# Six transformer layers on one core: the indexer's narrow columns share a block with the last values, the memory's values of two layers fill one block, its queries one tile

## The reference, cut to what matters

```python
# kind A; x is (256, 1024), all float32
q, k, v, qi, wi, ki, qm = split_cols(x @ w_in_a[j],
    (MIX_WIDTH, MIX_WIDTH, MIX_WIDTH, IDX_HEADS * IDX_DIM, IDX_HEADS, IDX_DIM, MEM_WIDTH))
...
ki = apply_rope(layer_norm(ki, idx_kn_g[j], idx_kn_b[j])[:, :, None, :], cos, sin)[:, :, 0]
mix = dsa_attention(q, k, heads(v, N_HEADS, HEAD_DIM), qi, wi, ki)
...
mk, mv = jnp.split(mem_n @ w_mem_kv[i], 2, axis=-1)
mo = memory_attention(heads(qm, ...), mk..., mv...)
mixed = jnp.concatenate([mix, mo], -1) @ w_out[i]
x = layer_norm(ALPHA * x + mixed, ...)
x = layer_norm(ALPHA * x + swiglu(x, w_gate_up[i], w_down[i]), ...)
```

## Time and profile before

| | us |
|---|---|
| median of 3 runs | 1611.58 (1610.95 to 1612.87) |
| the profiled execution, its own time | 1612.3 |
| its span, first to last instruction | 1610.5 |
| TensorE busy with matmuls | 1579.4 |
| VectorE busy | 1072.7 |
| ScalarE busy | 735.9 |
| mean granted TensorE clock | 0.993 |

### The profile page before, as it was taken

One profiled execution on the slowest core, in us unless ns is written; L12 is line 12 of the kernel. 1 busy time (PEld: TensorE's weight loads), 2 busy tenths in 40 slices (PEclk: granted clock), 3 DMA queues, 4 the chain that ended last, 5 costly groups with the idle time before them and its releaser, 6 DMA issues. The chain is left out here.

```text
span 1610.5 us, 20186 instructions
## 1 busy us (share of the span) xinstructions
PE 1579.4 (98%) x8390; PEld 1325.2 (82%) x8390; DVE 1072.7 (67%) x1403; ACT 735.9 (46%) x897; POOL 48.9 (3%) x89
## 2 busy tenths in 40 slices
PE   8999999999999999999999999999999999999998
PEld 6998888888878888888888888888888878887986
DVE  5784776756657767475766666766776668666754
ACT  5435444443434444345444443554444434564472
POOL 1100000000000000000000000000100000000000
PEclk9899999999999999999999999999999999999999
DMA  8552367564515666443367564522676546334530
GB/s 326 195 194 79 127 239 273 219 227 159 206 53 196 237 259 235 183 161 127 122 240 272 220 231 147 179 101 105 253 275 239 211 154 230 145 117 158 197 131 26
DMA packets 45179, 299.89 MB, mean 186 GB/s; under 512 B 5460, under 2 KB 5716, under 8 KB 11552
## 3 DMA queue, kind: packets, MB, share of 16 engines
q1 hardware_dynamic: 38880, 278.48, 46.6%
q0 software_dynamic: 5776, 19.01, 3.7%
q10 hardware_dynamic: 432, 1.11, 0.2%
HBM read 296.20 MB, written 2.65 MB: 186 GB/s over the span
## 5 line engine op out<-in xcount | busy, mean ns | idle before, releaser
L958 PE MATMUL psum<-w_high,xt_high 128*128 128x512 f32 (+2 forms) x1472 | 576.3, 392 | 10.6 <-DVE xt_low L1493 5.1
L1467 DVE TENSOR_TENSOR w_low<-w_raw,w_high 128x2048 fp32r<-128x2048 f32 (+1 forms) x240 | 544.5, 2272 | 44.9 <-ACT w_high L1287 43.7
L960 PE MATMUL psum<-w_high,xt_low 128*128 128x512 f32 (+2 forms) x1472 | 566.4, 385 | 0.0
L959 PE MATMUL psum<-w_low,xt_high 128*128 128x512 f32 (+2 forms) x1472 | 565.9, 384 | 0.0
L1287 ACT ACTIVATE w_high<-w_raw 128x2048 fp32r<-128x2048 f32 (+1 forms) x240 | 456.8, 1905 | 238.0 <-DMA w_raw<-in_weights 158.5
L958 PEld LDWEIGHTS psum<-w_high,xt_high 128*128 128x128 f32 x1472 | 279.1, 190 | 66.7 <-DVE w_low L1467 6.3
L960 PEld LDWEIGHTS psum<-w_high,xt_low 128*128 128x128 f32 x1472 | 279.0, 190 | 55.7
L959 PEld LDWEIGHTS psum<-w_low,xt_high 128*128 128x128 f32 x1472 | 279.3, 190 | 51.0
L1761 DVE TENSOR_TENSOR arena<-arena,psum 128x256 f32<-128x256 f32 x88 | 37.0, 420 | 206.5 <-ACT arena L1378 206.1
L958 PE MATMUL psum<-w_high,ht_high 128*128 128x512 f32 x352 | 140.8, 400 | 0.0
L960 PE MATMUL psum<-w_high,ht_low 128*128 128x512 f32 x352 | 137.5, 391 | 0.0
(11 more groups left out here) (230 smaller groups left out, 1608.8 us busy)
## 6 DMA issues: line engine op xcount, KB each, us to landing
w_raw<-in_weights SPq DMA_DIRECT2D x262, 1024.0 KB, 4.8
norm_params<-in_ln_g POOLq DMA_DIRECT2D x8, 512.0 KB, 4.1
norm_params<-in_ln_b POOLq DMA_DIRECT2D x8, 512.0 KB, 5.7
w_raw<-in_weights SPq DMA_DIRECT2D x4, 512.0 KB, 7.7
kv_outside<-arena POOLq DMA_DIRECT2D x3, 512.0 KB, 5.0
mem_kv<-kv_outside POOLq DMA_DIRECT2D x3, 512.0 KB, 3.7
norm_params<-mods_outside POOLq DMA_DIRECT2D x3, 512.0 KB, 5.8
x_rows<-in_x SPq DMA_DIRECT2D x2, 512.0 KB, 5.7
```

What stands on the lines that cost most here:

```text
L958: e.matmul(dst, a_hi, b_hi, start=first, stop=False)
L959: e.matmul(dst, a_hi, b_lo, start=False, stop=False)
L960: return e.matmul(dst, a_lo, b_hi, start=False, stop=last)
L1467: e.tensor_tensor(K.w_lo[:, s, 0:w], K.w_raw[:, r, 0:w], K.w_hi[:, s, 0:w].bitcast(F32), ALU.subtract).then_inc(K.taken.hit(t), 1)
```

## The change

1. In kind A the 72 narrow columns are laid beside the last 256 columns of the values: "beside", 328 columns, two tiles of 128 x 1312, at the place of narrow (line 595; in layer 3 line 603). VectorE copies the 8 and the 64 columns out as before, then ScalarE copies the 256 values (to two spare places in layer 0), and only that frees the bank.
2. The tail of kind A is gone. Its memory queries are one tile, "queries" (256 columns for all 1024 inputs), multiplied where the tail's turned half was; VectorE copies them out.
3. The memory's blocks are by pairs of layers, (1, 2) and (3, 0): a block of keys, 256 columns of each layer, turned, and a block of values, 512 columns wide with the rows standing, copied out in two instructions. The parks of layers 1 and 2 stand behind the first pair.
4. In kind A the attention's first unit starts a round earlier relative to the gemms (no step ahead in `headed`), and the transposes of the mix stand behind a round of units, not behind the gemm.

```diff
-BOTH = ("turned", "memory", "tail")
+BOTH = ("turned", "memory", "tail", "queries")
+BESIDE = MEMW + IDX_H + HD
+PAIRS = ((1, 2), (3, 0))
...
-        for layer in (*range(1, len(KINDS)), 0):
-            uses = [self.gemms.take() for _ in range(2)]
-            for half in range(2):
-                t = self.tile("w_mem_kv", layer, 0, "half", 4 * half)
...
+        for pair in PAIRS:
+            for part, sort in (("keys", "memory"), ("values", "block")):
+                uses = [self.gemms.take() for _ in range(2)]
+                for half in range(2):
+                    t = self.tile("w_mem_kv", pair, part, "pair", 4 * half)
+                    for n in range(2):
+                        self.gemm(t, n, half, ("mem",), "gemm", uses[n], sort)
+                        if half:
+                            self.evacuate((part, pair))(n, uses[n], t)
...
+        def beside(hooks):
+            uses = [self.gemms.take() for _ in range(RB)]
+            for half in range(2):
+                t = self.tile(w_in, at, None, "beside", 4 * half)
+                for rb in range(RB):
+                    self.gemm(t, rb, half, gen, "gemm", uses[rb], "beside")
+                    if half:
+                        beside_out(rb, uses[rb], t)
+                    hooks[half][rb]()
...
-            narrow([self.memory_rows(0), self.on])
+            beside([[self.on, self.on], [self.memory_rows(0), self.on]])
...
-        units = self.headed(own[0] + own[1][:ahead] + mem[:1] + own[1][ahead:] + mem[1:], 1 - ahead)
+        units = self.headed(own[0] + own[1][:ahead] + mem[:1] + own[1][ahead:] + mem[1:], 1 if kind == "C" else 0)
...
-        some(1, t_tail, ("tail", layer), "tail", [self.on, begin])
+        if kind == "A":
+            some(0, t_tail, ("qm", layer), "queries", [self.on, begin])
+        else:
+            self.blocks[("qm", layer), 0] = some(1, t_tail, ("tail", layer), "tail", [self.on, begin])
         some(0, t, ("proj", layer, 3), "block", [self.on] * 2)
-        some(0, t_tail, ("tail", layer), "tail", [self.on] * 2)
+        if kind != "A":
+            use = some(0, t_tail, ("tail", layer), "tail", [self.on] * 2)
...
         def first_turned():
+            if kind == "A":
+                self.step_background()
             if kind != "B":
                 self.xt(mix, 0, (0,))
-            self.on()
+            self.split() if kind == "A" else self.on()
...
-    if where == ("mem", 3):
+    if where[0] in ("keys", "values") and where[1] == PAIRS[1]:
         engine.wait_ge(*K.parked[1].at(0))
...
+    def evac_ki(j):
+        layer, rb, use, tile = j
+        act.wait_ge(*K.keys_out.at((layer, rb)))
+        e.activation(K.last_values(layer, rb), psum[:, K.gemms.place(use), 0:MEMW],
+                     ACT.Copy).then_inc(K.gemms.sem(use), 1)
```

More of the change, by code:

```diff
@@ L593, in queries, with beside_out @@
             return then
[L595 to L601, removed]
+        def beside_out(rb, use, t):
+            self.blocks[("v", layer), rb] = use
+            self.add("evac_ki", (layer, rb, use, t))
+        def beside(hooks):
[7 more added lines that the diff above has]
+                    hooks[half][rb]()
         def first_columns(more):
             halves = [self.tile(w_in, at, 3 * MIX, "half", 4 * half) for half in range(2)]
-            t, t_more = self.tile(w_in, at, None, "narrow", 0), self.tile(*more[:4], 0)
+            t = [self.tile(w_in, at, None, "beside", 4 * half) for half in range(2)]
+            t_more = self.tile(*more[:4], 0)
             uses_more = []
@@ L669, in attention @@
         self.group([keys], gen, [[self.on, keys_turned(0)], [self.step_background if late else self.on, keys_turned(1)]], True)
-        t_tail, t = [[self.tile(*what[:4], 4 * half) for half in range(2)] for what in (tail, values)]
+        if kind == "A":
+            t_tail = [self.tile(tail[0], tail[1], None, "queries", 0)] * 2
+        else:
+            t_tail = [self.tile(*tail[:4], 4 * half) for half in range(2)]
+        t = [self.tile(*values[:4], 4 * half) for half in range(2)]
         def some(n, tiles, where, sort, hooks):
@@ L1063, in gemm @@
             ring = K.gemms if j.ring == "gemm" else K.wide
-            halves = (0, 1) if j.kind == "narrow" else (j.half,)
-            bank, w = ring.place(j.use), IDX_H + HD if j.kind == "narrow" else BLK
-            if 0 in halves:
+            bank, half = ring.place(j.use), j.half
+            w = {"beside": BESIDE, "queries": SEQ}.get(j.kind, BLK)
+            if half == 0:
                 pe.wait_ge(*ring.free(j.use))
             rows_hi, rows_lo = (K.mt_hi, K.mt_lo) if j.gen[0] == "mem" else (K.xt_hi, K.xt_lo)
-            turned = j.kind == "turned" or (j.kind, rb) in (("memory", 0), ("tail", 1))
@@ L1636, in evac_ki @@
         layer, rb, use, tile = j
-        bank, rows = psum[:, K.gemms.place(use), :], K.idx[:, rb, :]
+        bank, rows = psum[:, K.gemms.place(use), MEMW:BESIDE], K.idx[:, rb, :]
         v.wait_ge(*K.multiplied.at((tile, rb)))
@@ L2241, in width @@
     def width(self, t):
[L2242 removed]
+        return KC // 2 * BESIDE if self.plan.tiles[t].what == "beside" else TW
     def part2(self, c):
@@ L2248, in kv_made, with kv_ready, last_values @@
         return self.kv_later[layer - 1] if layer else self.kv
+    def kv_ready(self, layer):
+        pair = next(pair for pair in PAIRS if layer in pair)
+        return [self.made(("keys", pair), pair.index(layer))] + [self.made(("values", pair), rb) for rb in range(RB)]
+    def last_values(self, layer, rb):
+        if layer == 0:
+            return (self.zeros32, self.ret_s[1][:, 0:MEMW])[rb]
+        return self.proj[:, rb, 4 * BLK:3 * MIX]
     def shift_row(self, layer):
@@ L2360, in pack_weights @@
             own = m[r, cols:cols + BLK]
-        elif what == "narrow":
+        elif what == "pair":
+            c0 = MEMW if cols == "values" else 0
+            own = np.concatenate([inputs[name][n][r, c0:c0 + MEMW] for n in layer], axis=1)
+        elif what == "beside":
             c0 = 3 * MIX + IDX_W
-            own = m[:, c0:c0 + IDX_H + HD]
+            own = np.concatenate([m[r, 4 * BLK:3 * MIX], m[r, c0:c0 + IDX_H + HD]], axis=1)
+        elif what == "queries":
+            own = m[:, m.shape[1] - MEMW:]
         elif what == "up":
```

149 lines of the change are left out of this document (84 added, 65 removed).

## The result

The changed kernel takes 1614.24 us (median of 20 runs, 1611.79 to 1617.16) against 1612.12 of the kernel before (20 runs, 1610.42 to 1614.46): ratio 1.0013 [1.0007, 1.0019], so 0.13% slower, where I had forecast 0.02% faster. Run again beside its variants it took 1615.16 us (11 runs) against 1612.26 (27 runs), ratio 1.0018 [1.0009, 1.0026]. The loss is small and real. It lies within the range and within the 0.2% that I called no change, but on the other side.

A forecast was written before the change was run, and what follows sets the result against it. TensorE's work was taken as the bound. Front +0.3, memory -0.8, layer 0 -2.4, layer 3 +1.8 and -1.0 gave -2.1; clock +1.7 made it -0.4: 1611.9 us, or 1611.2 against the median, range 1603 to 1617.

The forecast's parts named there:

- The rival of spacing by columns: All TensorE work: matmuls are spaced by columns alone, so the work does not shrink by 9.1; 1620.3 us, chance 0.02.
- the tail's -5.8: Layers 0 and 3, each: 48 matmuls of 256 columns for the values in the tail vanish, 5.8 us less.
- Front of layer 0: Up to the memory stage's start: a new 4.0 us wait for memt_low, start 0.5 later, clock 0.2 less lost; +0.3 us.
- Memory: Memory stage: 512-wide matmuls save 1.2 us, a wait behind VectorE's top-8 grows by 0.45, parks cost nothing; -0.8 us.
- (a): Attention of layers 0 and 3: TensorE waits for exps before turning the first probabilities, 0.4 and 1.8 us.
- (b): Attention of both layers: the first weighing waits for ScalarE's evacuation of ("proj", ., 3) behind a w_high, 1.7 us each.
- (c): Attention of both layers: transposes of the mix wait for a bank that VectorE's copy frees, 0.3 us twice.
- (d): Attention of both layers: the memory unit's weighing waits for ScalarE's last copy and a hand-over, 0.7 us.
- The rival that the covers hold: Attention: VectorE and ScalarE run ahead, so 5.6 us of waits and the slow clock stretch vanish; 1603.9 us, chance 0.22.
- Clock: One new stretch at half clock, expected from layer 3's attention waits: +1.7 us, with none to two giving 0 to 3.4.
- The slower rival: Slow clock lasts 10 us at layer 0's front and each attention has a stretch: +4.7, 1616.3 us, chance 0.20.
- +1.8: First columns of layer 3: 48 matmuls of 328 columns replace 96 of 72, 1.8 us more TensorE work.

The follow-up runs named there:

- the variant for the maxima: The changed kernel with VectorE's w_low behind, not ahead of, the first maxima of layer 3's attention; 1615.32 us, ratio 1.0021 to the kernel before.
- the second try: The changed kernel with w_low and w_high in layer 3's first columns, second row block, one step later; 1616.07 us, ratio 1.0019 to the kernel before.
- one w_low moved: The changed kernel with one w_low (tile 10) behind the two memt_low ahead of layer 0's memory stage; 1611.74 us, ratio 0.9996 to the kernel before.

## Why the prediction was wrong by 2.5 us

**TensorE's work: right.** The 328-wide matmuls, the one width that the trace of before lacked, are 0.15 us apart, as the straight line said (start and duration, us):

```profile
49.14 0.31 PE L990 MATMUL psum<-w_high,xt_low 128*128 128x328 f32 x1
49.29 0.32 PE L988 MATMUL psum<-w_high,xt_high 128*128 128x328 f32 x1
49.44 0.32 PE L989 MATMUL psum<-w_low,xt_high 128*128 128x328 f32 x1
49.59 0.32 PE L990 MATMUL psum<-w_high,xt_low 128*128 128x328 f32 x1
```

The rival of spacing by columns falls. Only the tail's -5.8 was a little too good: with the waits as measured (3.4 us) layer 0's attention gains 2.0 and not 2.4, so the work fell by 5.4. The formula in the section of the Trainium skill named above gives 0.139 for 328 columns, near to it, and 0.033 for the 72 that cost 0.112. I had read it for more than it says: the section gives it for an isolated matmul and warns that at few columns it counts too little where a weight load stands before each matmul, which this trace bears out. Its other warning, that at many columns the formula counts too much, does not hold here: 0.227 at 512 columns against the formula's 0.216. By the formula the whole edit would save 0.5 us (an estimate), and not the 0.4 that I wrote.

**Front of layer 0: mechanism right, times off.** I had VectorE's norm end at 52.1 (50.6 measured) and TensorE pass the block at 55.2 (52.6). I let the wait at 35 us (2.3 us) shrink by 0.5 where it vanished: with tiles of 1312 columns the second one is ready in time. The stretch at 1.2 GHz behind that wait vanished with it in this profile, and TensorE's lead grew by 1.6 us more over it (from 38 to 41.4 of the kernel before). The wait for memt_low behind two w_low came as forecast, 4.9 us for 4.0:

```profile
50.49 4.48 DVE L1506 TENSOR_TENSOR w_low<-w_raw,w_high 128x2048 fp32r<-128x2048 f32 x2
...
56.11 1.29 DVE L1532 TENSOR_TENSOR memt_low<-psum,memt_high 128x512 fp32r<-128x512 f32 x2 [0.94 <-ACT memt_high L1327]
...
57.54 0.55 PE L988 MATMUL psum<-memt_high,w_high 128*128 128x256 f32 x1 [4.94 <-DVE memt_low L1532]
```

By its end, 0.3 us ahead instead of 0.3 behind; the term is off by 0.3 to 0.6.

**Memory: right** (-0.8; -0.7 measured), with its 0.45 of wait and without cost from the parks.

**Attention: right in kind and size.** As distances of starts beyond the usual ones: (a) 0.4 and 1.8 forecast, 0.6 and 2.1 measured; (b) 1.7, and 1.6 twice; (c) 0.6, and 0.3; (d) 0.7, and 0.9. Moving the w_high removed (b) in both layers, and moving the w_low cut layer 3's (a) to layer 0's size, so these causes are shown and not only argued; (c) and (d) were not varied. The rival that the covers hold falls.

**Clock: wrong, in the kernel's favour.** I took one new stretch, +1.7. At the front it came as forecast, a stretch that begins in the wait (at 55.9) and ends near 62 (at 62.7; columns as in the earlier trace rows):

```profile
55.90:57.50 1.60, 0.00 (x0) 0.00 (x0) 1.39 (x4) 1.60 (x3) 0.00 (x0) 0.50 0.97 399
57.70:62.80 5.10, 5.10 (x25) 5.10 (x26) 2.29 (x1) 0.94 (x2) 0.00 (x0) 0.51 0.82 291
468.90:472.30 3.40, 3.37 (x10) 2.89 (x11) 1.81 (x5) 1.33 (x3) 0.00 (x0) 0.50 0.60 253
1325.70:1332.50 6.80, 6.19 (x15) 4.92 (x16) 6.66 (x10) 1.91 (x1) 0.52 (x1) 0.50 0.65 270
```

But the kernel before has 13.7 us at 1.2 GHz up to 62 us (3.4 of them behind its wait for weights at 35 us, which is gone), and the changed one 6.8 in both profiles: half of the 6.8 us between them, 3.4, saved where I had 0.2. That saving hides most of what the longer wait costs. In the attentions a stretch came in some executions only: in layer 3's none in the first profile and 3.4 us in the second, and in layer 0's, where I had expected none, two of 3.4 us each in the profiles of the variant for the maxima and of the second try, and one in that of one w_low moved. One that both kernels have at 1325 us is 3.4 us long in some and 6.8 in others. Over all runs the clock's part is 11.7 us and was 12.0. The slower rival put the loss on the clock, and it was not the clock. This error helped the forecast: without the clock I had -2.1, and work and waits came to +2.4, 4.5 us off, of which 2.0 (+1.7 forecast, -0.3 measured) were hidden by it. That the time lies within the range is in part luck.

**The step that failed** is "+1.8" for layer 3, the half of "layer 3 the same +1.8 and -5.8" that lies in the first columns. I priced the matmuls of that block and nothing else. For layer 0 I had followed what the second tile of the block does to VectorE's and ScalarE's queues; for layer 3 I did not, although the change adds a split there. That split brings one w_high and one w_low forward. The w_high waits for a tile still on its way and holds ScalarE's copies; the w_low stands ahead of the indexer keys. It cost 1.3 and 2.1 us in the two profiles, the largest error in work and waits that both of them have. How the cost divides between the w_high and the w_low is open (the w_high has 0.4 to 1.2 of it), and no variant turned this wait into a gain of time.

**A second, smaller omission:** a lead was not always kept. In the first profile 0.9 us of layer 0's lead goes by 243 us, the most of it at a wait for the bank that VectorE's product in the feed-forward frees; that product waits for ScalarE, which is just behind a w_high that had waited 3.1 us for its tile. Small waits of the kind stand at 842 and 1170 us. In the second profile, and with the w_high moved in the attention, the one at 238 us is missing. It seems to depend on how the tiles' arrival falls against TensorE; that was not tested, and what decides it stays open.

Together, in the first profile's stages against the forecast's: front -0.6, memory +0.1, the two attentions +0.4 and +0.5, layer 3's queries and keys +1.3, leads given back +1.8 (two of about 1.1 and 0.7), the clock behind them 1.4 where 1.7 was forecast in all: from -0.4 to +2.8. A slip in the text of the sum: "new waits of some 10 us" are 12.7 by its own terms (4.0, 0.45, 3.4 and 4.8); the forecast was not made from that figure.

## What to carry over

When a change takes work off the bound engine, list at each place that it touches what the other engines' queues gain or lose there, prefetch steps included: here 8 to 9 us of TensorE's work were all returned because waits of 0.3 to 5 us opened, most of them behind a rounding step (w_high or w_low, 2 us) whose result nobody needed yet. Moving such steps at three places behind the copy or evacuation that TensorE waits for turned 0.13% slower into 0.46% faster than before. Judge one such move together with the next wait of its chain: alone, the maxima's gave nothing.

## What the runs showed of the hardware

- The clock's part of the same program, span times (1 - mean clock), varies from run to run by 1 to 2 us (one standard deviation). Within a kernel the span grows by 0.56 us for each microsecond of it, so taking it off whole makes kernels with unequal clock's parts look more different, or less, than they are.
- A wait does not decide by itself whether the clock falls. The 2.0 us wait for the exps in layer 3's attention stands in seven profiles. In two of them the clock fell to 1.2 GHz for 3.4 us within 1 us of its end, in a third 8 us later, behind the next wait, and in four not at all there. TensorE's wait of 4.0 us at about 1320 us stands in every profile of every kernel, and 3.4 us at 1.2 GHz go with it in some and 6.8 in others.
- How long TensorE waits for its first weights at 31 us differs between two executions of the changed kernel by 1.7 us (2.1 and 3.8), and a stretch at 1.2 GHz followed the longer wait. TensorE then reached the memory rows 3.0 us later and the stage behind the next wait only 1.3 us later, as much as VectorE's norm was later (50.41 against 49.16): VectorE's queue, not TensorE's arrival, sets that point.
